# Attention pairs of a hybrid transformer block: the order of maxima, copies and inverse sums around the probability product

## The reference: what is computed

```python
def softmax_attend(q, k, v, sink):
    s = jnp.einsum('bqgrd,bkgd->bgrqk', q, k).astype(jnp.float32) * (q.shape[-1] ** -0.5)
    ...
        p = jax.nn.softmax(s, axis=-1)
    ...
    return jnp.einsum('bgrqk,bkgd->bqgrd', p.astype(v.dtype), v)
```

## Time and profile before

| what | value |
|---|---|
| median of 3 runs | 2508.59 us (2500.33 to 2518.37) |
| the profiled execution's own time | 2509.4 us |
| its span, first to last instruction | 2507.6 us |
| TensorE busy | 2271.5 us, 91% of the span |
| VectorE, ScalarE, GpSimd busy | 1012.0, 678.7 and 807.8 us |
| mean granted TensorE clock | 0.937 of full speed |
| attention stages | about 302 to 492 us (layer 0), 1677 to 1826 us (layer 1) |
| one latent block | 36.4 us |

### The profile page before, as it was taken

One profiled execution on the slowest core, in us unless ns is written; L12 is line 12 of the kernel. 1 busy time (PEld: TensorE's weight loads), 2 busy tenths in 40 slices (PEclk: granted clock), 3 DMA queues, 4 the chain that ended last, 5 costly groups with the idle time before them and its releaser, 6 DMA issues.

```text
span 2507.6 us, 45977 instructions
## 1 busy us (share of the span) xinstructions
PE 2271.5 (91%) x19350; PEld 1827.1 (73%) x19350; DVE 1012.0 (40%) x1473; ACT 678.7 (27%) x1181; POOL 807.8 (32%) x570
## 2 busy tenths in 40 slices
PE   5999888889989799999999699988888988999997
PEld 3888556459967588888888478845657866788885
DVE  3000555474653741514132430055546654632443
ACT  3001355642221211111111221135552222221221
POOL 3332243013122423223232544124303225344443
PEclk8999999978999799999999789899987999999998
DMA  6122000120011222211212322200030013233331
GB/s 248 58 70 97 34 1 0 34 89 3 4 60 56 79 63 64 63 62 59 67 59 63 139 74 93 81 34 1 0 115 10 4 61 119 82 101 92 94 99 59
DMA packets 45404, 162.42 MB, mean 65 GB/s; under 512 B 5504, under 2 KB 5504, under 8 KB 45024
## 3 DMA queue, kind: packets, MB, share of 16 engines
q1 hardware_dynamic: 44480, 157.89, 19.1%
q0 software_dynamic: 800, 2.69, 0.3%
HBM read 158.46 MB, written 2.10 MB: 64 GB/s over the span
## 4 chain that ended last, share of the span: by engine, by line
PE 79%; DVE 12%; ACT 4%; issue 2%; DMA 1%; POOL 1%; SPq 0%; POOLq 0%; DVEq 0%; ACTq 0%
PE ps L1333 75%; PE ps L1584 2%; DVE small L1087 1%; DVE part_h L985 1%; DVE hT L978 1%; DMA flat<-wmod_dram 1%; DVE xT L1003 1%; DVE flat L1317 1%; ACT flat L755 1%; DVE ps L1084 1%; POOL flat L517 1%; ACT flat L737 1%; DVE flat L1001 0%; PE ps L1846 0%; DVE flat L1067 0%
## 5 line engine op out<-in xcount | busy, mean ns | idle before, releaser
L1333 PE MATMUL ps<-part_hi,wparts 128*128 128x512 f32 (+1 forms) x3072 | 816.3, 353 | 26.7 <-DVE part_h L985 8.1
L1333 PEld LDWEIGHTS ps<-part_hi,wparts 128*128 128x128 f32 x3072 | 545.9, 191 | 116.1 <-DVE part_h L985 14.2
L498 POOL TENSOR_TENSOR wparts<-flat,wparts 128x1024 fp32r<-128x1024 f32 x184 | 442.4, 2404 | 544.8 <-ACT wparts L914 539.0
L1333 PE MATMUL ps<-flat 64*64 64x32 f32 (+8 forms) x8812 | 497.7, 266 | 71.8 <-ACT flat L755 30.4
L1333 PEld LDWEIGHTS ps<-flat 64*64 64x64 f32 (+4 forms) x8812 | 386.4, 148 | 168.7 <-issue 74.8
L1333 PE MATMUL ps<-part_h,wparts 128*128 128x512 f32 (+1 forms) x1344 | 474.3, 353 | 0.0
L1333 PE MATMUL ps<-part_mlp,wparts 128*128 128x512 f32 (+1 forms) x1536 | 417.7, 359 | 4.5 <-DVE part_h L985 4.5
L1333 PE MATMUL ps<-part_lo,wparts 128*128 128x512 f32 x960 | 342.1, 356 | 0.0
L1333 PEld LDWEIGHTS ps<-part_mlp,wparts 128*128 128x128 f32 x1536 | 275.3, 191 | 52.7 <-DVE part_h L985 11.2
L914 ACT ACTIVATE wparts<-flat 128x1024 fp32r<-128x1024 f32 x112 | 118.8, 1061 | 704.3 <-PE ps L1333 704.3
L1333 PEld LDWEIGHTS ps<-part_h,wparts 128*128 128x128 f32 x1344 | 257.9, 192 | 31.8 <-issue 0.2
(11 more groups left out here) (198 smaller groups left out, 2056.7 us busy)
## 6 DMA issues: line engine op xcount, KB each, us to landing
flat<-w_dram SPq DMA_DIRECT2D x128, 512.0 KB, 3.6
flat<-wmod_dram SPq DMA_DIRECT2D x94, 512.0 KB, 5.2
flat<-win_dram SPq DMA_DIRECT2D x40, 512.0 KB, 3.6
flat<-wout_dram SPq DMA_DIRECT2D x16, 512.0 KB, 3.7
xT<-xT_dram SPq DMA_DIRECT2D x8, 384.0 KB, 6.7
flat<-rope_dram SPq DMA_DIRECT2D x2, 1024.0 KB, 5.7
out_dram<-xT SPq DMA_DIRECT2D x8, 256.0 KB, 2.0
flat<-wmask_dram SPq DMA_DIRECT2D x2, 768.0 KB, 7.2
```

Of the source, the lines that this page charges most:

```text
L498: pool.tensor_tensor(wlo[q % 2], src, whi[q % 2], ALU.subtract).then_inc(s_used[q], 1)
L1333: return pe.matmul(out, lhsT, rhs, start=start, stop=stop)
```

## The change

Four edits, all in the attention trips, and in every trip of latent and context blocks alike unless said otherwise.

1. VectorE: both maxima, of heads 2p+2 and 2p+3, now stand ahead of the copy of head 2p+1, which stood between them.
2. ScalarE: in trips 1 and 2 (latent scores) the exponentials of head 2p+2 stand ahead of the copy of head 2p+1. The copy of the spread inverse sums (`over_sum`) now stands behind the copy of 2p+1 in all trips, and waits for `normed` of the trip before, which reads `over_sum`.
3. TensorE: `spread_sums(p)` stands behind `turns(2p+1)`, ahead of `output(p)`. It no longer waits for `normed(p-1)`; `output(p)` now waits for that, and no longer for the copy `over_sum` of its own trip.
4. The spread inverse sums go to PSUM column 3584 (bank 7) and no longer to 3200 (bank 6, beside the output).

```diff
--- before.py
+++ after.py
@@ -176,7 +176,7 @@
         kwin = zT[:, C_KV * TOK:C_KV * TOK + 384]
 
         mix = hT[:, 4 * TOK:6 * TOK].rearrange("p (b f) -> p b f", b=NB)
-        O_AT, SPREAD_AT = 3072, 3072 + P
+        O_AT, SPREAD_AT = 3072, 3584
         ROWS_OF = (0, 2, 1, 3, 0, 1, 2, 3, 0, 2, 1, 3)
         TILE_OF = (0, 1, 2, 3, 6, 7)
 
@@ -755,12 +755,20 @@
                             nc_.activation(probT[:, h % 2, 0:w], ps[:, 2048:2048 + w], ACT.Copy).then_inc(s_pta, 1)
 
                         for p in range(6):
+
+                            def exps_of(h):
+                                exps(h % 12, at + (12 if h >= 12 else 0))
+
                             turned(2 * p)
+                            if p in (1, 2):
+                                exps_of(2 * p + 2)
+                            turned(2 * p + 1)
                             act.wait_ge(s_spr, i * 6 + (turned0 // 2 + p + 1))
+                            act.wait_ge(s_on, 1 + i * 6 + (turned0 // 2 + p))
                             nc_.activation(over_sum, ps[:, SPREAD_AT:SPREAD_AT + P], ACT.Copy).then_inc(s_spre, 1)
-                            turned(2 * p + 1)
-                            for h in (2 * p + 2, 2 * p + 3):
-                                exps(h % 12, at + (12 if h >= 12 else 0))
+                            if p not in (1, 2):
+                                exps_of(2 * p + 2)
+                            exps_of(2 * p + 3)
                             if p % 2:
                                 act.wait_ge(s_S, 1 + at + 4 * (p // 2 + 1))
                                 queries(p // 2, i * P + P if b0 == 0 else (b0 + 1) * P - i * P)
@@ -1128,9 +1136,8 @@
                             turned(2 * p)
                             inverse_sums(p)
                             for h in (2 * p + 2, 2 * p + 3):
-                                if h % 2:
-                                    turned(2 * p + 1)
                                 peak(h % 12, at + (12 if h >= 12 else 0), i)
+                            turned(2 * p + 1)
                             normed(p)
                         ch.leave(n)
 
@@ -1587,7 +1594,6 @@
                         def spread_sums(p):
 
                             pe.wait_ge(s_sum, pairs + (p + 1))
-                            pe.wait_ge(s_on, 1 + pairs + p)
                             for g in range(2):
                                 c = 16 + 2 * p + g
                                 ins = mm(ps[64 * g:64 * g + 64, SPREAD_AT:SPREAD_AT + P],
@@ -1598,7 +1604,7 @@
 
                             pe.wait_ge(s_pta, 1 + done + (2 * p + 2))
                             pe.wait_ge(s_ptd, 1 + done + (2 * p + 2))
-                            pe.wait_ge(s_spre, pairs + (p + 1))
+                            pe.wait_ge(s_on, 1 + pairs + p)
                             grp = p // 2
                             if win and p == 4:
                                 pe.wait_ge(s_vw, i + (NBL * l + 1))
@@ -1625,8 +1631,8 @@
                             if win and p == 3:
                                 pe.wait_ge(s_kw, i + (NBL * l + 1))
                             scores((p + 1) % 6, at + (2 * p + 2), i + (asked + (1 if p == 5 else 0)))
+                            turns(2 * p + 1)
                             spread_sums(p)
-                            turns(2 * p + 1)
                             output(p)
 
                 ring_row(4)
```

## The result

The changed kernel takes 2529.55 us, the median of 7 runs from 2525.28 to 2536.44, beside 2506.86 us for 7 runs of the kernel before: a ratio of 1.0102, with a 95% interval from 1.0074 to 1.0130 (the two medians alone give 1.0091). I had forecast 2563 us, within 2524 to 2592. The sign and the mechanism of the queue were right, the size was not: the time is that of my rival 1 (2528 us). It is slower by 1.0%, not by 2.2%.

What follows compares the result with a forecast made beforehand. TensorE was taken to bound the latent trips and VectorE the windowed ones. From 2509.4 us, +20 (queue, net of gains), -1 (context blocks) and +36 (clock) gave 2564, less 0.8 for the median: 2563 us, range 2524 to 2592.

Steps and rivals of the forecast that it cites:

- the mechanism of the queue: VectorE's strict FIFO: a copy whose input is ready cannot pass the maxima; +20 us over eight latent blocks, net of gains.
- rival 1: Only VectorE's queue costs time, the clock stays untouched: 2528 us, +0.8%; chance 0.17.
- Spread sums and latent trips: Trips 1 and 2: spread sums fall into TensorE's 0.69 us wait for copies, gaining 0.37 us each.
- the late copy: Latent trips: VectorE reaches its copy some 0.2 us late, beside ScalarE's copy; the full 0.37 us gain was still taken.
- Windowed trips and trips of A: Copy behind both maxima costs +1.5 us in trip 3, +1.35 in trip 4, 0 in trip 5, +0.44 in trip 0.
- The context blocks: Second maximum fits beside the transposes, gain mostly kept in A and B: 0 to -2 us for two blocks, taken as -1.
- The clock: TensorE's longer gaps in trips 3 and 4 drop the clock behind most of them: 4.5 us a block, +36 us.
- my bound: Trips 3 to 5: 9 us a block if the clock stays low until trip 0, 0 if it never falls.
- The row with 2.60 us idle: Earlier trace: clock 0.60 in the 3.2 us after 2.60 us idle, taken as nearest to the new gaps.
- The first exponential and the bank: ScalarE's first exponential fits ahead of the latent transposes; the spread sums' own PSUM bank costs nothing and allows the new order.

Runs made afterwards that it cites:

- the one-edit kernels: VectorE's two maxima put ahead of the second head's copy in the kernel before: 2541.99 us; that order undone in the changed kernel: 2484.21 us.
- the fillers: Changed kernel plus unused dummy matmuls on TensorE ahead of the output in trips 3 and 4 of latent blocks: three, 2518.97 us; five, 2532.42 us.
- the kernel with the order alone: Kernel before with only VectorE's two maxima moved ahead of the second head's copy, in all trips: 2541.99 us, 1.0117 times the kernel before.

## Why the prediction was right and wrong

- **Spread sums and latent trips: right.** -0.43 us for a forecast of -0.37, and this closeness is in part luck, since two terms were out: the place of the spread sums gave 0.52 us and not 0.37 (the kernel with them alone), and the late copy, which I had put at nothing there, took 0.08 us of it back. The waits that were moved show no cost.
- **Windowed trips and trips of A: right.** +1.56, +1.32, -0.13 and +0.42 us for +1.5, +1.35, 0 and +0.44. The block was to grow by 2.55 us and grew by 2.30; over eight blocks this is 17 to 18 us (the first of each layer grows by 2.0, the last of layer 0 by 1.8), for a forecast of 20. The idle time ahead of the outputs was forecast at 2.6 and 2.5 us and is 2.60 and 2.45 us. That the copy is what TensorE waits for is shown by both the one-edit kernels, 2542 and 2484 us.
- **The context blocks: right in size where the clock is alike.** The second one went from 17.80 to 17.29 us, at 1.00 both times. The first gained 4.4 us, most of it by the clock (0.77 there before, 1.00 now), which is luck of these two profiles.
- **The clock: the step that failed.** I wrote "I take half, 4.5 us" a block, 36 us in all. The mechanism is there, and the fillers show its price: 10.6 us by the times, 12.2, some 15 and 10.6 us by the blocks of three profiles (two of them the changed kernel, the third the one without the first exponential in front). That is 1.3 to 1.9 us a block and not 4.5. Two things were missized. I took it that the clock falls "behind most of them": it fell behind 6, 9 and 6 of the 16 gaps, in four to six of eight blocks. And a fall cost less than the 3.1 us behind trip 3 and the 6 us behind trip 4 of my bound: 1.6 us where only one came, 2.9 to 4.5 us where both did, not 9, because by the second set of transposes behind the gap the clock was back. The row with 2.60 us idle that I leaned on the earlier trace rows had thin work on both sides, and here the gap had dense matmuls on both. Whether that is the reason isn't shown: in the kernel with the order alone the same gaps brought falls in all eight blocks, and in that with the late copy in the windowed trips alone in seven. What decides whether a gap brings a fall stays open.
- **Rival 1 and the total.** The time came out as rival 1's 2528 us, but by another sum than rival 1 told: 17.5 us of queue, some 12 us of clock, and in this pair of profiles 4.9 us back in the context blocks. The attention of these two profiles grew by 24.6 us with that, and the time by 22.7 us. So "clock untouched" was no more true than the forecast. The first exponential and the bank, which I had put at nothing, were measured at nothing.

## What to carry to other kernels

Two edits that look like one idea can have opposite signs: here the spread sums moved behind the transposes gain 0.9%, and a copy moved behind two maxima turns that into a loss of 1.0%. On an in-order queue, put an instruction that another engine is already waiting for ahead of work whose result is wanted later, and look trip by trip: the same order cost 0.08 us in the latent trips, where the first maximum runs while TensorE still computes scores (from 394.66 us, scores until 395.75), some 0.8 us in those of A, where both maxima start behind the scores (from 388.74 us, scores until 388.64), and 1.3 to 1.6 us where they carry a mask. The version to keep is the changed kernel with VectorE's old order, or the spread sums alone: 2484 and 2485 us, against 2507 before and 2530 with the change.

## What the runs showed of the hardware that I had not expected

- Adding useless matmuls in an idle stretch of 2.5 us made the kernel 10.6 us faster (2518.97 for 2529.55 us), since the clock then stayed at 1.00. With fillers longer than the gap (3.49 us) the gain was gone.
- The same idle gap of 2.60 us was followed by a stretch with a clock of 0.50 in one block and of 1.00 in the next, in one execution. In that block the clock was still 1.00 up to 369.00 us, 1 us behind the gap's end, and the lower level showed for part of one output, one set of transposes and one set of scores. Behind the gap of trip 4 it was there from 375.80 us, before the gap's end.
- Where the work is thin, as in the context blocks, the kernel before has the clock at 0.77 and 1.00, and the kernel with the bank alone at 0.54 over 27 us and at 0.73 over the next 23 us, for the same instructions in the same order.
